# A hybrid SSD, attention and mixture-of-experts block on one core: the attention heads taken in pairs, norm2 loads issued during them, and GpSimd dividing their rows

## What is computed

```python
# gqa_mixer: 16 query heads, 4 key/value heads, head size 64; queries are the 256 latent tokens,
# keys and values are 256 latent + 256 context tokens
q, k, v = split(a @ w_qkv)
q = rope(rms_norm(q, q_gain)); k = rope(rms_norm(k, k_gain))
p = softmax(q @ k.T * HEAD_DIM ** -0.5)          # rows of 512, per head
m_l = (p @ v) @ w_o
x_lat = x_lat + g1 * m_l
f_l = rms_norm(x_lat, norm2_g) * (1 + sc2) + sh2   # norm2, then the routing of the MoE
y = hier_moe(f_l, w_group, b_group, w_router, b_router, w_gate, w_up, w_down)   # 32 experts
x_lat = x_lat + g2 * y
```

## Time and profile before

| what | value |
|---|---|
| median of 3 runs | 1873.03 us (1872.93 to 1875.63) |
| the profiled execution | 1872.92 us, of which the span of its instructions 1871.1 us |
| granted TensorE clock, mean | 0.956 of full speed |
| busy: TensorE, VectorE, ScalarE, GpSimd | 1562.1, 535.0, 415.9, 254.1 us |

### The profile page before, as it was taken

The page is one execution under the profiler, slowest core; times in us unless marked ns, Lnnn a source line. Parts: engine busy times, 40 slices in busy tenths (PEclk is TensorE's granted clock), DMA queues, the critical chain, the costliest instruction groups (busy, mean ns, idle before and its releaser), DMA issues.

```text
span 1871.1 us, 21703 instructions
## 1 busy us (share of the span) xinstructions
PE 1562.1 (83%) x8634; PEld 825.4 (44%) x8634; DVE 535.0 (29%) x1134; ACT 415.9 (22%) x827; POOL 254.1 (14%) x267
## 2 busy tenths in 40 slices
PE   3999999999999889788877773977789888777774
PEld 2434446666545555444434341433455544434341
DVE  2433347777533320000000003455331000000001
ACT  2221147888501101000000002145110100000000
POOL 2000013443210101010101002100110110101001
PEclk9899999999999999999999997978889999999997
DMA  9477759995342799999999996710469999999994
GB/s 362 159 287 285 271 198 256 309 318 207 125 161 78 279 396 421 421 421 422 421 421 421 422 419 237 271 49 1 167 267 382 419 419 421 420 422 420 420 421 178
DMA packets 166141, 579.74 MB, mean 310 GB/s; under 512 B 22290, under 2 KB 77986, under 8 KB 143296
## 3 DMA queue, kind: packets, MB, share of 16 engines
q1 hardware_dynamic: 145072, 531.25, 71.8%
q0 software_dynamic: 15248, 27.62, 4.3%
q10 hardware_dynamic: 5760, 20.06, 3.3%
HBM read 550.60 MB, written 49.77 MB: 321 GB/s over the span
## 4 chain that ended last, share of the span: by engine, by line
PE 48%; DMA 38%; DVE 6%; issue 3%; ACT 3%; POOL 1%; SPq 0%; ACTq 0%; POOLq 0%; DVEq 0%
DMA mem<-in_moe_w_down_dram 33%; PE bank L588 9%; PE bank L1777 8%; PE bank L1764 7%; PE bank L937 6%; PE bank L882 3%; PE bank L2027 3%; PE bank L331 2%; PE bank L905 2%; DMA mem<-in_mod_w_dram 2%; DMA mem<-in_moe_w_gate_dram 1%; ACT mem L987 1%; PE bank L2053 1%; PE bank L900 1%; PE bank L2133 1%
## 5 line engine op out<-in xcount | busy, mean ns | idle before, releaser
L1764 PE MATMUL bank<-mem 128*64 128x256 f32 x4160 | 475.2, 383 | 86.0 <-DMA mem<-in_moe_w_up_dram 38.5
L1764 PEld LDWEIGHTS bank<-mem 128*64 128x64 f32 x4160 | 304.4, 137 | 257.0 <-DMA mem<-in_moe_w_up_dram 59.8
L1777 PE MATMUL bank<-mem 128*64 128x512 f32 x1040 | 254.3, 634 | 89.9 <-DMA mem<-in_moe_w_down_dram 80.7
L1920 DVE COPY mem<-bank 128x256 f32<-128x256 f32 x65 | 27.6, 425 | 690.4 <-PE bank L1771 690.4
L1715 POOL DMA_INDIRECT ys_dram<-mem x65 | 64.7, 996 | 864.8 <-ACT mem L1870 491.1
L1777 PEld LDWEIGHTS bank<-mem 128*64 128x64 f32 x1040 | 76.0, 144 | 226.0 <-issue 132.9
L1870 ACT ACTIVATE mem<-bank 128x512 f32<-128x512 f32 x65 | 38.8, 597 | 611.4 <-PE bank L1777 611.4
L588 PE MATMUL bank<-mem 128*128 128x512 f32 x384 | 173.1, 604 | 1.4 <-DMA mem<-in_ssd_w_in_dram 1.4
L588 PEld LDWEIGHTS bank<-mem 128*128 128x128 f32 x384 | 71.8, 192 | 100.0 <-issue 96.8
L882 PE MATMUL bank<-mem 128*128 128x512 f32 x256 | 115.2, 593 | 0.0
L937 PE MATMUL bank<-mem 128*128 128x512 f32 x256 | 112.3, 595 | 1.8 <-issue 0.9
(11 more groups left out here) (277 smaller groups left out, 1430.3 us busy)
## 6 DMA issues: line engine op xcount, KB each, us to landing
mem<-in_moe_w_up_dram SPq DMA_DIRECT2D x65, 2048.0 KB, 27.3
mem<-in_moe_w_down_dram SPq DMA_DIRECT2D x65, 2048.0 KB, 26.8
mem<-in_moe_w_gate_dram SPq DMA_DIRECT2D x65, 2048.0 KB, 26.4
mem<-in_mod_w_dram SPq DMA_DIRECT2D x24, 2048.0 KB, 8.9
ys_dram<-consts SPq DMA_DIRECT2D x54, 512.0 KB, 7.8
mem<-in_ssd_w_in_dram SPq DMA_DIRECT2D x10, 2048.0 KB, 9.4
mem<-ac_dram ACTq DMA_DIRECT2D x32, 512.0 KB, 5.5
mem<-in_ssd_w_out_dram SPq DMA_DIRECT2D x4, 2048.0 KB, 11.8
```

Of the source, the lines that this page charges most:

```text
L1764: mm = nc.tensor.matmul(bank[half * BR:(half + 1) * BR, 0:HF], lhsT=x[:, k], rhs=w[:, k, half * HF:(half + 1) * HF], start=(k == 0), stop= ...
L1777: mm = nc.tensor.matmul(bank[half * BR:(half + 1) * BR, :], lhsT=ht[:, k % 2, k // 2 * BR:(k // 2 + 1) * BR], rhs=w[:, k, half * COLS:(hal ...
```

## The change

In attention the step j is a pair of items (two heads of one tile), 16 steps in all. `scores`, `top`, `turn`, `Exp` and `turned` handle two items at a time. `share(j)` on VectorE makes only the two reciprocals; GpSimd multiplies the rows (`share_pool`). Half of `project(1, 1)` moves behind the first scores, both `turn_q` of queries 8 to 15 move into the loop, and `values(7)` moves into the output projection. An `Exp` of one element stands ahead of attention's work on ScalarE. `norm2_pool` for layer 1 no longer waits for the end of attention: gain, `wrt` and `mA` go to other places in memory and are loaded between the shares; `brt` and `mB` are loaded after the last share. `norm2_prep_dve` (formerly `prep` and `shift_sums`) stands ahead of the last `output`. In layer 0 the same loads and the same work stand in another order.

```diff
-        mA = region(M0 + 2048, 2048, "p (s d) -> p s d", s=2)
-        mB = region(M0 + 4096, 2048, "p (s d) -> p s d", s=2)
+        mA = [region(M0 + at, n * D, "p (s d) -> p s d", s=n) for at, n in ((2048, 2), (7168, 1))]
+        mB = [region(M0 + at, n * D, "p (s d) -> p s d", s=n) for at, n in ((4096, 2), (10240, 1))]
...
             else:
-                pool.wait_ge(at_o, QH // 2)
+                pool.wait_ge(at_q, 4)
             mod_wait(pool, NG if l else MODG)
+            pool.dma_start(wrt[l][:, :, 0:EG], a["moe_w_group"][l].rearrange("(k p) n -> p k n", p=P)).then_inc(n2_in, 16)
+            pool.dma_start(wrt[l][:, :, EG:], a["moe_w_router"][l].rearrange("(k p) n -> p k n", p=P)).then_inc(n2_in, 16)
             pool.dma_start(gain2, a["norm2_g"][l:l + 1, :].to_broadcast([P, D])).then_inc(n2_in, 16)
...
+            for s in range(ns):
+                pool.dma_start(mA[l][:, s, :], mod_dram[l, s:s + 1, 4 * D:5 * D].to_broadcast([P, D])).then_inc(n2_in, 16)
+            if l:
+                for i in range(4, NI2):
+                    share_pool(pool, i)
+                pool.wait_ge(n2_in, N2_IN[1][0])
+                pool.wait_ge(at_s, 2 * QH)
...
+        N2_IN = [(16 * 9, 16 * 9), (16 * 13, 16 * 16)]
...
             for n, cols in enumerate([*Q_COLS[0:2], *K_COLS, *Q_COLS[2:4]]):
+                if n == 7:
+                    for i in range(4):
+                        share_pool(pool, i)
                 pool.wait_ge(at_ms, n + 1)
...
+        def share_pool(pool, i):
+            pool.wait_ge(at_inv, i // 2 + 1)
+            nc.gpsimd.tensor_scalar(prob[:, i % 4, :], prob[:, i % 4, :], ainv[:, i:i + 1], None, ALU.mult).then_inc(
+                at_n, 1)
...
+            def scores(j):
+                p, t = divmod(j, 2)
+                if j >= 2:
+                    pe.wait_ge(at_p, 2 * j - 2)
...
+            def turn(j):
+                for hh in range(2):
+                    pe.wait_ge(at_n, 2 * j + hh + 1)
+                    if j:
+                        pe.wait_ge(at_pe, 2 * j + hh - 1)
...
+            project(1, 1, 5, range(4))
             pe.wait_ge(at_te, 6)
...
+            scores(0)
+            scores(1)
+            project(1, 1, 5, range(4, KD))
+            for j in range(NJ):
+                if j + 2 < NJ:
+                    if j + 2 == NJ // 2:
+                        pe.wait_ge(at_te, 8)
+                    scores(j + 2)
+                if j in (0, 3):
+                    turn_q(2 + j // 3)
+                turn(j)
+                if j >= 2 and j % 2 == 0:
+                    if j <= 4:
+                        pe.wait_ge(at_te, 6 + j // 2)
+                    values(j // 2 - 1)
...
+            out_part(0, 0, range(NPAIRS - 2))
+            values(NPAIRS - 1)
+            pe.wait_ge(at_o, NPAIRS - 1)
+            out_part(0, 0, [NPAIRS - 2])
+            pe.wait_ge(at_o, NPAIRS)
+            out_part(0, 0, [NPAIRS - 1])
...
+            nc.scalar.activation(craw[:, 0, 0:1], mhalf[:, 0:1], ACT.Exp)
...
+            for j in range(NJ):
+                if j >= 1 and j + 1 < NJ:
+                    exps(j + 1)
+                turned(j)
+                if j in (0, 3):
+                    turned_q(2 + j // 3)
...
+            def share(j):
+                dve.wait_ge(at_p, 2 * j + 2)
+                V.reciprocal(ainv[:, 2 * j:2 * j + 2], asum[:, 2 * j:2 * j + 2]).then_inc(at_inv, 1)
...
+            for j in range(NJ):
+                share(j)
+                if j == 1:
+                    query_mean(3)
+                    query_turn(3)
+                if j + 2 < NJ:
+                    top(j + 2)
+                if j >= 3 and j % 2:
+                    output((j - 3) // 2)
+            norm2_prep_dve(dve, 1)
             output(NPAIRS - 1)
```

More of the change, by code:

```diff
@@ L1390, in norm2_dve @@
             iota_e = consts[:, C_E:C_E + E]
[L1392 to L1412, removed]
             def shift_rows():
                 dve.wait_ge(rt_shift, 2 * l + 2)
+                dve.wait_ge(n2_in, N2_IN[l][1])
                 c2 = psum[7][:, 384:384 + ns * NR].rearrange("p (s n) -> p s n", s=ns)
@@ L2035, in turn_q @@
                     c = (4 * u + r) * P
[L2036 removed]
+                    tp = nc.tensor.transpose(psum[Q_AT[j]][:, r * P:(r + 1) * P], qrow[:, t, c:c + P], ident)
                 tp.then_inc(at_tp, 1)
@@ L2270, in key, with top @@
                 dve.wait_ge(at_k, t + 1)
[L2272 to L2281 removed]
+            def top(j):
+                c = pair_cols(j)
+                for hh in range(2):
+                    i = 2 * j + hh
+                    dve.wait_ge(at_s, i + 1)
+                    ins = V.tensor_reduce(amax[:, i:i + 1], psum[SB[j % 2][hh]][:, :], AX, ALU.max)
+                link(dve, ins)
+                if j >= NJ // 2:
+                    dve.wait_ge(at_rs, 7 + j % 2)
+                V.scalar_tensor_tensor(abias[:, 2 * j:2 * j + 2], amax[:, 2 * j:2 * j + 2], -1.0, qk_rs[:, c:c + 2],
+                                       ALU.mult, ALU.mult).then_inc(at_m, 1)
+            def share(j):
+                dve.wait_ge(at_p, 2 * j + 2)
+                V.reciprocal(ainv[:, 2 * j:2 * j + 2], asum[:, 2 * j:2 * j + 2]).then_inc(at_inv, 1)
             def output(p):
@@ L2302, in attn_dve @@
             stream_rows_dve(dve, 1)
-            query(0)
+            query_mean(0)
+            query_turn(0)
             stream_evac_dve(dve, 1)
-            query(1)
+            query_mean(1)
+            query_turn(1)
             for t in range(NT):
                 key(t)
-            query(2)
-            dve.wait_ge(at_rs, 7)
+            query_mean(2)
+            query_turn(2)
             top(0)
             top(1)
-            for i in range(NI2):
-                if i == 5:
-                    query(3)
-                    dve.wait_ge(at_rs, 8)
-                if i + 2 < NI2:
-                    top(i + 2)
-                share(i)
-                if i >= 4 and i % 4 == 3:
-                    output(i // 4 - 1)
+            for j in range(NJ):
[8 more added lines that the diff above has]
+            norm2_prep_dve(dve, 1)
             output(NPAIRS - 1)
```

196 lines of the change are left out of this document (86 added, 110 removed).

## The result

| what | before | after | forecast |
|---|---|---|---|
| median, same chip (runs) | 1873.9 us (1872.93 to 1875.63, 4) | 1855.8 us (1854.19 to 1857.48, 4) | 1836 us (1827 to 1850) |
| ratio, 95% interval | | 0.9902 [0.9885, 0.992] | 0.980 |
| profiled execution, span | 1872.92, 1871.1 us | 1854.19, 1852.2 us | |
| first Exp of attention | 1228.25 | 1224.64 | 1224.6 |
| loop over (first of `w_o`) | 1319.31 | 1309.41 | 1290.2 |

The kernel became faster by 18 us; I had forecast 37. The direction was right, and the time lies above my range. The first expert starts 19.1 us earlier and the span is 18.9 us shorter, so all of it is won ahead of MoE 1, as forecast. The first expert comes 18.0 us later than I had put it: 19.2 us were lost up to the end of the head loop, and 1.2 us were won behind it.

The account below looks back on a forecast made before the run. MoE 1 was taken as transfer-bound, so only starting it earlier, after a shorter head loop and no pause behind it, helps: 35.4 us to the sums over partitions plus 1.7 gives 37.1 off 1872.92, 1836 us (1827 to 1850).

Parts of the forecast that it names:

- the price of the share: Head loop: one GpSimd multiplication of a 512-wide row estimated at 0.8 us, with 0.49 and 1.53 as ends.
- the circle: Head loop, per head pair: values, scores, maxima, scaling, reciprocal, two shares, transposes; 7.4 us, before 0.5 for the clock.
- The row at 1.53 us: Rival in the head loop: shares cost as much as GpSimd's dearest product, with small operands; 1847 us, chance 0.15.
- The estimate of 0.43 us a share: Head loop: by the Trainium skill's line-rate claim, 0.43 us and dispatch a share, the kernel 4 to 5 us lower.
- the clock: Head loop: TensorE's time at its lower clock level adds 0.5 us a circle, 3.3 us in all.
- the transposes of step 2: Start of the head loop: after query(3), loads and shares, these transposes end at 1239.6.
- The 11.2 us a pair: Head loop of the kernel before: 22 items counted in 61.71 us, from 1247.31 to 1309.02.
- The early loads: Behind the loop: loads and tables made earlier remove TensorE's 8.18 us pause; products after the sums gain 1.7 us.
- The way behind the loop: From the loop's end to the sums over partitions: products and values take 15.95 us, without a pause.
- GpSimd at its dearest row: Rival in the head loop: each share takes 1.53 us, 8.8 us more in six circles; 1847 us, chance 0.15.
- wait for its code: Rival at the loop's start: GpSimd's first share delayed by up to 10.4 us of code loading; 1843 us, chance 0.08.
- The lower clock for the whole loop: Rival in the head loop: TensorE at its lower level throughout, 11.2 us a pair; 1857 us, chance 0.07.

Follow-up runs that it names:

- e3: Changed kernel with GpSimd's share written as a product of two tensors, the reciprocal broadcast along the row: 1839.4 us, ratio 0.9826.
- e4: Changed kernel with 12 and 6 extra transposes of constants on TensorE ahead of the share waits of even steps: 1847.2 us, ratio 0.9864.
- e5: Changed kernel with VectorE making the reciprocals of step j + 1 ahead of the maxima of step j + 2: 1838.9 us, ratio 0.9824.
- e2: Kernel before with only layer 1's early norm2 loads and tables, head loop as before: 1863.1 us, ratio 0.9951.
- e1: Changed kernel with the shares back on VectorE, all else as changed: 1829.1 us, ratio 0.9759.
- e10: Changed kernel with the shares on VectorE and norm2's loads and tables back behind the loop: 1838.8 us, ratio 0.9822.
- e6: Changed kernel with each step's first share on GpSimd and its second on VectorE: 1840.0 us, ratio 0.9829.

## Why the prediction was wrong

**The step that failed** is the price of the share: "reading one tensor costs it 0.487/0.68 = 0.72 of reading two; I put the same ratio on 1.13 and take 0.8 us". It measured 1.59 us in the mean and 1.55 in the circle. The ratio was VectorE's, and GpSimd goes the other way: its form with one tensor is dearer than that with two (1.59 against 1.06 in e3). Even my upper end, 1.53, lay below it. Two shares cost 1.5 us a circle more than I took, 9 us over six circles. The row at 1.53 us, which I had named and given 0.15, came near, but by luck. It is a product of two tensors with a broadcast operand, and 1.53 is a mean: its 16 instructions took 1.03 to 2.02 us, median 1.49, and both other groups of products have the same least time, 1.03, with a median of 1.04. So undisturbed products cost 1.03 us, with a small operand or without, as e3's do; the mean of 1.53 is the spread of these rows and not the price of a small operand (what lengthens some of them I have not tested). The trace of before had no row for the form that the change uses. The estimate of 0.43 us a share that the prediction gives beside its sum is not borne out either: no share took less than 1.55.

**The term that was mis-sized with it** is the clock: "TensorE will be busy 80% of a circle instead of 65%, so I take 0.5". The figures of 80 and 65% are TensorE's 6.2 us of work at full clock in 7.9 and 9.56 us; in 10.4 us it is 60%, so the circle got emptier and not fuller. (By busy time in the trace it was 77% before, 53.06 of 69.00 us, and 73% after.) TensorE waited 2.4 us for the shares in each circle; e4 measured the clock at 1.6 us a circle. That is 1.1 more than I took, near 7 us. The two terms are not independent, as e3 shows: the cheaper share took both away.

**The rest of the loss, by place.** Until the transposes of step 2 the loop lost 3.4 us (1243.0 against 1239.6), as the four shares, then 1.74 us of factors, loads and two more shares stand in one queue. About 1.6 of them are the factors of query(3), which my sum did not have ahead of the loads, and 1.5 the price of step 2's two shares; the rest is the slower turn. Six circles of 10.4 instead of 7.9 lost 15.1, the end of the loop 0.7: together the 19.2 us between 1290.2 and 1309.4.

**A miscount that the sum does not use.** The 11.2 us a pair of the kernel before come from 22 items where the trace has 23; over like steps it is 10.4 us, as shown above. No term of the 37.1 us is worked out from it, but it made the loop look as if shorter circles were to be won, and the measured circles won none.

**What was right.** The structure: the circle through both shares, transposes, values, scores, maxima and reciprocals, and what ends it. e5 confirmed that VectorE's order closes it. The start (first Exp 1224.64). The early loads (e2: 10.8 us against 9.9 in the sum) and no waiting for `mB`. The way behind the loop, 15.8 us against 15.95. The shift of MoE 1 one to one: from the last transposes ahead of its first expert (1376.94 before, 1357.63 after) to the end of the span it is 493.1 to 494.8 us in before, after, e1 to e5 and e10. The extra Exp and layer 0's new order showed no cost.

**The rivals.** GpSimd at its dearest row was the right mechanism. That its 1847 us was also the time of e4 is in part luck: its circle, with 0.5 us of clock, would be 9.4 us, and e4's is 8.8. The first share did not wait for its code (1226.57, as forecast). The lower clock for the whole loop did not come, since scores ran at full clock (1.11 us) and only what follows the pause was slow. Neither rival alone gives 1855.8; the cause joins a part of each. My range ended at 1850 because I had counted them as exclusive.

## What to carry to other kernels

Price an operation by rows of the same engine and the same form, and look at their least and median times: a mean can mix undisturbed rows with lengthened ones. Where no row has the form, say so and keep the range wide; here a ratio taken from another engine pointed the wrong way. Where one operand is small beside a wide tensor, write the operation also as a product with a broadcast operand and compare. When work moves to a slower engine on a circle that TensorE is part of, count two terms: TensorE's longer wait, and the clock that may fall behind it (here 1.6 us a circle, for waits that were 1.1 us longer than those of e3). Count the circle of the kernel before with care, over like steps: here it was 10.4 us before and 10.4 us after, so the loop's circles gained nothing. What freed an engine is worth only what that engine's share of the circle was: here the VectorE that was relieved had been busy 38 of 69 us, and the version that leaves the shares with it, 1829 us, beats both kernels.

## What the runs showed of the hardware

**GpSimd.** `tensor_scalar` with one scalar a partition, 128 x 512 in 32 bits, took 1.55 us undisturbed; `tensor_tensor` with the same operand broadcast 1.03 (2.05 for two), the same as the least time of products of two wide tensors; VectorE's `tensor_scalar` 0.49. The first share began 0.27 us after its reciprocal had begun, 0.1 after its end, and took 1.57 us. No loading of code showed there; the engine's two configuration rows stand at 1221.8, ahead of 4.74 us of idle time, so a delay shorter than that could be hidden.

**Two engines on one memory.** Beside VectorE's multiplication of 0.49 us GpSimd's share took 1.86 us in the median and the mean (e6), and 1.9 beside the products of query(3) in the changed kernel; in e6, where both stood beside one share, it took 2.38. The Trainium skill (SBUF — State Buffer, "Who interferes with whom") says that VectorE in a mode with two ports, or with two inputs from SBUF against a GpSimd operation that reads it, contends with GpSimd for a shared pair of ports, and that whichever is first holds the pair for its whole instruction while the other is fully blocked. The runs agree in direction, with 0.3 us longer; by my estimate a full block by an operation of 0.49 us that began 0.06 us earlier would be 0.43. No row names VectorE's mode.

**The clock.** With TensorE idle for 1.55 and 0.88 us in each circle, on either side of 0.66 us of transposes, the granted clock of the stretch was 0.83: 1.00 in the part that holds the waits (1256.8 to 1263.0), 0.59 in the 4.2 us behind them, where the second transposes and the values ran slow (1.1 and 3.1 us). With the waits filled, or at 1.01 and 0.34 us, the clock of the stretch was 0.99 and 1.00 and they took 0.66 and 1.88. One idle time of 3.00 us in e1 had the same effect once.
